# A two-layer decoder trunk on one core: feature-major input and memory, the first weights in quarters, the memory handled late in the first FFN

## The chip, the cores and the metric

The kernel runs on one core of one Trainium2 chip. The metric is the device time of one execution in microseconds (us). The core has a matrix engine (TensorE, PE in the profile), a vector engine (DVE), a scalar engine (ACT), GpSimd (POOL), and a sync engine (SP) that issues most of the DMAs. ACT and POOL can issue DMAs as well. Each engine works through its own instructions in order; semaphores tie the engines together.

## The reference

The input `x` is 256 tokens by 1024 features in f32, and there is a second input `mem` of the same shape. Two layers follow, each of four sub-layers with an RMSNorm ahead and one behind:

```
x += 1/2 * post(SwiGLU_1(pre(x)))          FFN, 1024 -> 2816 -> 1024
x += post(Mixer_l(pre(x)))                 layer 0: MLA | mLSTM, layer 1: sparse attention
x += post(CrossAttn(pre(x), norm(mem)))    4 heads over the 256 rows of mem
x += 1/2 * post(SwiGLU_2(pre(x)))
```

with `rmsnorm(x, g) = x * rsqrt(mean(x*x) + eps) * g` and `swiglu(x) = (silu(x @ wg) * (x @ wu)) @ wd`. The change concerns the first sub-layer (the first FFN) and the norm of `mem`, which the cross-attention of both layers uses.

## The kernel before, in words

**Products.** Each f32 operand is split in two: `hi` is the operand rounded to the matrix engine's f32r type, `lo` is the rest. A product is three terms: hi x hi, hi x lo, lo x hi. ACT makes `hi` (`hi_half`, a copy with a cast), DVE makes `lo` (`lo_half`, a subtraction). For the gate and up products of an FFN, `h_hi` and `h_lo` lie side by side in `h_both`, so one instruction of 512 columns does hi x (hi, lo) and one of 256 columns does lo x hi.

**Weights.** They come in chunks of 1 MB (128 partitions x 2048). SP loads a chunk into one of three raw slots (`raw` has two, `QT` is the third inside an FFN); ACT and DVE split it into a ring of four places, `w_ring`. `load(c)` on SP waits until the `lo` split of the slot's chunk before is done. An FFN has 11 pairs of gate and up chunks (G0.0, U0.0, ... in the text; the first digit is the sub-layer) and 11 down chunks (D0.0 ...). The order of work is written out by hand, on every engine: G0.0, U0.0, then for each pair p: G0.(p+1), U0.(p+1), D0.p. The middle eight turns are a hardware loop (`Fori`). At the end stand G0.10, U0.10, then D0.9 and D0.10 by token tiles, so that the first 128 tokens come out earlier.

**Input.** `pre` is not applied ahead of the first product: the gain goes into the input split, the row factor `rstd` is applied to the sums. It is put on a diagonal (`rdiag`), a product with a matrix of ones spreads it over the partitions (`row_factors` on PE, `rbc`), and `gate_scale` on DVE multiplies by it. The matrix engine needs features on the partitions, and `x` is loaded with tokens on the partitions, so PE turns the 16 blocks of 128x128 (`input_transposes`, L1072 of the profile). Ahead of them stand 13 transposes of nothing (`idle_turns`, L1253) and one that turns the norm gains (L1258). Then ACT makes `h_hi` (`input_hi`, L1579) and DVE `h_lo` (`input_lo`, L2243). `first_gate` runs G0.0 by halves of the features (L818 for `hi`, L823 for `lo`), `first_up` runs U0.0 (L861, L865).

**Memory.** `mem` is loaded with tokens on the partitions into `KTs` (`stage`), squared on ACT, scaled by DVE (L2234), turned by PE between U0.0 and G0.1 (`memory_transposes`, L1114) and split from PSUM in `m_hi` (ACT, `mem_hi`, L1698) and `m_lo` (DVE, `mem_lo`, L2429). Small parameter vectors come in nine small DMAs and are turned by one PE transpose (L1106) into `pcol`. The first user of the split memory is `fill(1)`, the product xk0.0, right behind the first FFN. Its weights are scaled by the memory's gain out of `pcol` while they are split: eight ACT instructions (L1543) and eight DVE instructions (L2205). Behind the FFN, `boundary` on DVE splits xk0.0 first, then multiplies the FFN's output by its gain (`gained`, L2257), adds it to x (`residual`, L2267), scales the rows (L2234), and makes the next `h_lo` (L2243), for which the first mixer product on PE (L755) waits.

**Order in the last pair of the first FFN.** ACT: `silu(10)`, the split of xk0.0, then `act_hi(10)`, the `hi` of the last activations. DVE: `gate_scale(10)`, the split of D0.10, `gate_up(10)`, `act_lo(10)`, then `boundary`. PE waits for `act_lo(10)` before the last down product (`act_ready(p)`).

## Time and profile before

| | |
|---|---|
| device time, median of three runs | 1104.31 us (1104.12 to 1104.64) |
| span of the profiled execution | 1102.8 us |
| PE busy | 1088.2 us, 99% of the span |
| DVE busy | 775.5 us, 70% |
| ACT busy | 562.1 us, 51% |
| POOL busy | 65.1 us, 6% |
| chain that ended last | PE 88%, DVE 6%, ACT 3% |

The span is that of one profiled execution, from its first to its last instruction; no device time of its own is given for that execution, and the median of the runs lies 1.5 us above its span. Line numbers are those of the kernel before. A matmul's row shows the time from its start to its modelled end; matmuls overlap, so the chain's rows, which follow the ends, are shorter than the durations of single ones.

### The profile page before, as it was taken

The page shows a single profiled execution, that of the slowest core. Times are in us where ns is not written, and L with a number is a line of the kernel's source. Part 1 is how long each engine was busy: PE and PEld are TensorE (multiplying, and loading weights), DVE is VectorE, ACT ScalarE, POOL GpSimd, SP SyncE. Part 2 cuts the span into 40 slices and gives each one's busy share as a digit, 9 for nine tenths or more (in the row PEclk, how much of TensorE's full clock was granted, in tenths as well). Part 3 has the DMA queues.
Part 4 walks back from the last instruction along what each step waited for, and adds up shares of the span by engine and source line. Part 5 has one row for each costly group of instructions (what it writes and reads, how often), then busy time and mean ns, then how long its engine had stood idle before and what let it go on. Part 6 is the DMA issues. An engine that isn't in the chain of part 4 may idle for free.

```text
span 1102.8 us, 16056 instructions
## 1 busy us (share of the span) xinstructions
PE 1088.2 (99%) x6175; PEld 941.6 (85%) x6175; DVE 775.5 (70%) x1023; ACT 562.1 (51%) x817; POOL 65.1 (6%) x168
## 2 busy tenths in 40 slices
PE   8999999999999999999999999999999999999997
PEld 7888888997889888888888888888987988888886
DVE  6867666763877677766768776677488768776674
ACT  7544344645667764434455443445465765443442
POOL 4000000210011010000010000001100101000000
PEclk9999999999999999999999999999999999999999
DMA  8655553571244356455426655552904435645540
GB/s 298 247 204 185 187 200 115 173 253 39 79 152 173 134 229 229 167 187 217 161 106 248 229 191 190 191 181 86 305 1 153 148 139 211 229 164 189 218 153 38
DMA packets 49399, 192.98 MB, mean 175 GB/s; under 512 B 3302, under 2 KB 24748, under 8 KB 31036
## 3 DMA queue, kind: packets, MB, share of 16 engines
q1 hardware_dynamic: 47932, 187.87, 48.3%
q0 software_dynamic: 1264, 4.25, 1.1%
q8 instruction: 38, 0.62, 0.2%
q14 instruction: 21, 0.17, 0.0%
q10 hardware_dynamic: 144, 0.07, 0.0%
HBM read 191.12 MB, written 1.05 MB: 174 GB/s over the span
## 4 chain that ended last, share of the span: by engine, by line
PE 88%; DVE 6%; ACT 3%; issue 1%; DMA 1%; POOL 0%; POOLq 0%; DVEq 0%; ACTq 0%
PE psum L878 28%; PE psum L978 21%; PE psum L877 12%; PE psum L1204 4%; PE psum L963 3%; PE psum L881 2%; PE psum L1195 1%; DVE w_ring L2211 1%; PE psum L742 1%; PE psum L744 1%; PE psum L743 1%; PE psum L767 1%; PE psum L769 1%; PE psum L768 1%; PE psum L818 1%
## 5 line engine op out<-in xcount | busy, mean ns | idle before, releaser
L878 PE MATMUL psum<-h_both,w_ring 128*128 128x512 f32 x1328 | 460.6, 396 | 0.0
L877 PE MATMUL psum<-h_both,w_ring 128*128 128x256 f32 x1162 | 324.0, 279 | 0.0
L2211 DVE TENSOR_TENSOR w_ring<-raw,w_ring 128x2048 fp32r<-128x2048 f32 x120 | 274.1, 2285 | 31.3 <-ACT w_ring L1547 31.0
L878 PEld LDWEIGHTS psum<-h_both,w_ring 128*128 128x128 f32 x1328 | 240.3, 188 | 46.5
L1547 ACT ACTIVATE w_ring<-raw 128x2048 fp32r<-128x2048 f32 x121 | 231.8, 1916 | 78.7 <-PE psum L978 48.6
L2335 DVE TENSOR_REDUCE work<-psum 128x256 f32<-128x512 f32 x174 | 118.4, 687 | 177.6 <-PE psum L878 176.5
L877 PEld LDWEIGHTS psum<-h_both,w_ring 128*128 128x128 f32 x1162 | 219.1, 189 | 7.4
L978 PE MATMUL psum<-w_ring,g_both 128*128 128x512 f32 x936 | 219.2, 389 | 0.0
L978 PEld LDWEIGHTS psum<-w_ring,g_both 128*128 128x128 f32 x936 | 175.7, 188 | 35.4
L1645 ACT ACTIVATE V<-work 128x512 f32<-128x512 f32 x44 | 27.8, 632 | 181.7 <-DVE work L2344 181.7
L2211 DVE TENSOR_TENSOR w_ring<-QT,w_ring 128x2048 fp32r<-128x2048 f32 x40 | 91.3, 2283 | 1.1 <-ACT w_ring L1547 1.0
L1649 ACT ACTIVATE g_both<-V 128x512 fp32r<-128x512 f32 x43 | 27.2, 633 | 120.5 <-DVE V L2351 120.5
L1547 ACT ACTIVATE w_ring<-QT 128x2048 fp32r<-128x2048 f32 x40 | 76.2, 1905 | 0.5 <-DMA QT<-in_ffn_w_down 0.5
L881 PE MATMUL psum<-h_both,w_ring 128*128 128x256 f32 x166 | 46.1, 277 | 0.0
L2243 DVE SCALAR_TENSOR_TENSOR h_both<-psum,gcol,h_both 128x128 fp32r<-128x128 f32 x128 | 34.6, 343 | 12.5 <-ACT h_both L1579 12.0
L638 POOL TENSOR_SCALAR part<-ss,eps_in 128x1 f32<-128x1 f32 x8 | 2.5, 312 | 692.4 <-ACT V L1569 692.4
L1579 ACT ACTIVATE h_both<-psum,gcol 128x128 fp32r<-128x128 f32 x128 | 35.1, 389 | 12.2 <-PE psum L1072 12.2
L881 PEld LDWEIGHTS psum<-h_both,w_ring 128*128 128x128 f32 x166 | 31.2, 188 | 6.8
L742 PE MATMUL psum<-h_both,w_ring 128*128 128x256 f32 x128 | 36.9, 288 | 0.0
L744 PE MATMUL psum<-h_both,w_ring 128*128 128x256 f32 x128 | 36.2, 283 | 0.0
L743 PE MATMUL psum<-h_both,w_ring 128*128 128x256 f32 x128 | 36.2, 283 | 0.0
L978 PE MATMUL psum<-w_ring,h_both 128*128 128x512 f32 x144 | 35.0, 396 | 0.3 <-DVE h_both L2174 0.2
(307 smaller groups left out, 1451.6 us busy)
## 6 DMA issues: line engine op xcount, KB each, us to landing
raw<-in_ffn_w_up SPq DMA_DIRECT2D x44, 1024.0 KB, 4.8
raw<-in_ffn_w_gate SPq DMA_DIRECT2D x43, 1024.0 KB, 4.8
QT<-in_ffn_w_down SPq DMA_DIRECT2D x40, 1024.0 KB, 4.7
raw<-in_ab_w_in SPq DMA_DIRECT2D x9, 1024.0 KB, 5.4
gain_row<-in_norm_g POOLq DMA_DIRECT2D x8, 512.0 KB, 5.0
raw<-in_ffn_w_down SPq DMA_DIRECT2D x4, 1024.0 KB, 4.7
raw<-in_xa_wk SPq DMA_DIRECT2D x4, 1024.0 KB, 4.8
raw<-in_ab_w_out SPq DMA_DIRECT2D x4, 1024.0 KB, 5.0
```

What stands on the lines that cost most here:

```text
L742: nc.tensor.matmul(o, wh, a_hi[:, k, :], start=(k == 0), stop=False)
L743: nc.tensor.matmul(o, wh, a_lo[:, k, :], start=False, stop=False)
L744: last = nc.tensor.matmul(o, wl, a_hi[:, k, :], start=False, stop=(k == KT - 1))
L877: nc.tensor.matmul(out_[:, 0:TOK], lo[:, k, o], h_hi[:, k, :], start=False, stop=False)
L878: last = nc.tensor.matmul(out_[:, :], hi[:, k, o], h_both[:, k].rearrange("p a n -> p (a n)"), start=(k == 0), stop=(k == KT - 1))
L881: nc.tensor.matmul(out_[:, 0:TOK], lo[:, k, o], h_hi[:, k, :], start=False, stop=False)
L978: last = nc.tensor.matmul(psum[:, 2 * t + half, :], a, w[:, k, 512 * half:512 * (half + 1)], start=(first and k == 0 and a is ah and w is hi),
L1204: last = nc.tensor.matmul(out_[0:rows, cols], a, b, start=(n == 0), stop=(n == len(terms) - 1))
L1547: nc.scalar.activation(w_hi[:, c % RING, 0:k * n], raw_at(c)[:, 0:k * n], ACT.Copy)\
L1579: ins = nc.scalar.activation(h_hi[:, k, P * t:P * (t + 1)], turned_at(s, t, k), ACT.Copy, scale=gain(s, k))
L2211: nc.vector.tensor_tensor(w_lo[:, c % RING, 0:k * n], raw_at(c)[:, 0:k * n], w_hi[:, c % RING, 0:k * n].bitcast(F32), ALU.subtract).then_i ...
L2335: nc.vector.tensor_reduce(dst[:, p % 2, TOK * j:TOK * (j + 1)], bank(name).rearrange("p (a n) -> p n a", a=2), AX.X, ALU.add)\
```

## The change

**Input.** The host lays out four more arrays: `first` (the gains of the first norm and `x`, feature-major), `gain_cols` (all norm gains by column), `mem_turned` (memory feature-major) and `columns` (the parameter vectors and `mem_norm_g` by column). The input and gain transposes on PE are gone. SP loads `first` in four DMAs of about 256 KB, ACT's queue loads G0.0 in four of 256 KB, and U0.0 comes in two halves on SP, ahead of `gcol`. `x` with tokens on the partitions is loaded behind G0.1, by two DMAs of 512 KB ahead of that of U0.1.

**First products.** ACT and DVE split input and weights quarter by quarter (two feature blocks each), out of SBUF and not out of PSUM. PE runs G0.0 in four steps and U0.0 in two (`by_steps`), and G0.1 by `first_up`, which starts on `hi` alone. 16 idle transposes stand ahead of it all.

**Memory.** Both layouts of `mem` are loaded at the end of the loop of the first FFN. The squares come ahead of the last but one pair on ACT. DVE puts the row factors on a diagonal, PE spreads them by one product (`memory_factors`, between G0.10 and U0.10), ACT copies them out, DVE multiplies the turned memory by them, ACT makes `m_hi` and DVE `m_lo`, all inside the last pair. PE's transposes of the memory and of the parameters are gone.

```diff
-            for t in range(NT):
-                sp.dma_start(x[:, t, :], A['x'][0, P * t:P * (t + 1), :]).then_inc(x_load[t], 16)
...
+            for q in range(4):
+                o = slice(KT + 2 * TOK * q if q else 0, KT + 2 * TOK * (q + 1))
+                sp.dma_start(work[:, o], A['first'][:, o]).then_inc(first_x_load[q], 16)
+            for half in range(2):
+                o = slice(4 * half, 4 * (half + 1))
+                dst = raw[:, 1, :].rearrange("p (k n) -> p k n", k=KT)
+                sp.dma_start(dst[:, o, :], chunks[1][1][0][:, o, :]).then_inc(raw_full[1] if half else first_up_load, 16)
+            sp.dma_start(gcol[:, :], A['gain_cols']).then_inc(gain_load, 16)
...
+            def load_memory():
+                sp.dma_start(stage, A['mem'][0].rearrange("(t p) n -> p t n", p=P)).then_inc(mem_load, 16)
+                sp.dma_start(m_raw[:, :, :], A['mem_turned']).then_inc(mem_turned_load, 16)
+                sp.dma_start(pcol[:, 0:NP], A['columns']).then_inc(par_load, 16)
...
-                for c in range(max(c0, 1), c1):
+                for c in range(max(c0, 2), c1):
                     load(c)
-                    if c == 1:
-                        sp.dma_start(stage, A['mem'][0].rearrange("(t p) n -> p t n", p=P)).then_inc(mem_load, 16)
-                        load_parameters()
+                    if c == 2:
+                        for t in range(NT):
+                            sp.dma_start(x[:, t, :], A['x'][0, P * t:P * (t + 1), :]).then_inc(x_load[t], 16)
...
+            def by_steps(name, ks, input_waits, hi_waits, lo_waits):
...
+                for step, (on_input, on_hi, on_lo) in enumerate(zip(input_waits, hi_waits, lo_waits)):
+                    if on_input:
+                        pe.wait_ge(*on_input)
+                    pe.wait_ge(*on_hi)
+                    for j in range(2):
+                        for k in range(ks * step, ks * (step + 1)):
+                            nc.tensor.matmul(outs[j][:, :], hi[:, k, P * j:P * (j + 1)],
+                                             h_both[:, k].rearrange("p a n -> p (a n)"), start=(k == 0), stop=False)
+                    pe.wait_ge(*on_lo)
...
+                def memory_factors():
+                    pe.wait_ge(mdiag_done, NT)
+                    filled("mrow", nc.tensor.matmul(take("mrow")[:, 0:TOK], ones[:, :], mdiag, start=True, stop=True))
...
# ACT, first FFN
+                if s == 0:
+                    act.wait_ge(mem_load, 16)
+                    for t in range(NT):
+                        square("m", t, stage[:, t, :], unread=m_hi[:, :, :].rearrange("p (t a) n -> p t (a n)", t=NT))
                 triple(p - 1)
                 nxt[0] = c0 + 3 * PAIRS - 1
                 split_to(nxt[0])
+                if s == 0:
+                    evacuate("mrow", mrow, bank("mrow")[:, 0:TOK])
                 silu(p)
+                if s == 0:
+                    mem_hi()
+                    act.wait_ge(par_load, 16)
                 split_to(c0 + 3 * PAIRS)
...
# DVE, first FFN
                 gate_scale(p)
                 split_to(nxt[0])
+                if s == 0:
+                    mem_scale()
...
                     gate_up(p)
                     act_lo(p)
+                if s == 0:
+                    mem_lo()
+                    dve.wait_ge(mem_split, 2)
                 boundary(s, C[f"D{s}.{p}"])
```

The first place is the start of ACT, which splits the first input and weights. In these rows `h_both` is the split input, `w_ring` the split weights, `KTs` the memory. Before:

```order
L1776 DMA work<-in_norm_g 128x128
L1560 ACT_TABLE_LOAD
L1560 ACTIVATE gcol<-psum 128x128
L1579 ACTIVATE h_both<-psum,gcol 128x128 x8
L1783 ACTIVATE w_ring<-raw 128x1024
L1579 ACTIVATE h_both<-psum,gcol 128x128 x8
L1787 ACTIVATE w_ring<-raw 128x1024
L1547 ACTIVATE w_ring<-raw 128x2048
L1569 ACTIVATE V,ss<-x_state 128x1024 x2
L1569 ACTIVATE V,ss<-KTs 128x1024 x2
L1547 ACTIVATE w_ring<-raw 128x2048 x2
L1698 ACTIVATE m_hi<-psum 128x512 x4
```

And changed:

```order
L1791 DMA raw<-in_ffn_w_gate 128x512 x4
L1795 ACT_TABLE_LOAD
L1795 ACTIVATE h_both<-work 128x256 x2
L1799 ACTIVATE w_ring<-raw 128x512
...
L1795 ACTIVATE h_both<-work 128x256 x2
L1799 ACTIVATE w_ring<-raw 128x512
L1803 ACTIVATE w_ring<-raw 128x1024 x2
L1553 ACTIVATE w_ring<-raw 128x2048
L1575 ACTIVATE V,ss<-x_state 128x1024 x2
L1553 ACTIVATE w_ring<-raw 128x2048
```

Eight passes over the input of twice the width stand in place of sixteen, in turn with the quarters of G0.0; the memory's six instructions are gone from here.

The second place is ACT at the end of the first FFN, from the split of D0.10 on (`g_both` is the last activations, `lat` holds the spread factors, `pcol` marks the split of xk0.0). Before:

```order
L1547 ACTIVATE w_ring<-raw 128x2048
L1645 ACTIVATE V<-work 128x512
L1543 ACTIVATE w_ring<-raw,pcol 128x256 x8
L1649 ACTIVATE g_both<-V 128x512
L1569 ACTIVATE V,ss<-psum 128x512 x2
```

And changed:

```order
L1553 ACTIVATE w_ring<-raw 128x2048
L1566 ACTIVATE lat<-psum 128x256
L1651 ACTIVATE V<-work 128x512
L1710 ACTIVATE m_hi<-KTs 128x1024 x2
L1549 ACTIVATE w_ring<-raw,pcol 128x256 x8
L1655 ACTIVATE g_both<-V 128x512
L1575 ACTIVATE V,ss<-psum 128x512 x2
```

The memory's two `hi` passes stand ahead of the split of xk0.0, and both ahead of the `hi` of the last activations.

The third place is DVE in the same stretch, from the split of D0.10 on. Before:

```order
L2211 TENSOR_TENSOR w_ring<-raw,w_ring 128x2048
L2335 TENSOR_REDUCE work<-psum 128x256 x2
L2351 TENSOR_TENSOR V<-V,work 128x512
L2356 TENSOR_TENSOR g_both<-V,g_both 128x512
L2205 SCALAR_TENSOR_TENSOR w_ring<-raw,pcol,w_ring 128x256 x8
L2257 TENSOR_TENSOR KTs<-psum,gain_row 128x512 x2
```

And changed:

```order
L2224 TENSOR_TENSOR w_ring<-raw,w_ring 128x2048
L2449 TENSOR_TENSOR KTs<-m_raw,lat 128x1024 x2
L2348 TENSOR_REDUCE work<-psum 128x256 x2
L2364 TENSOR_TENSOR V<-V,work 128x512
L2369 TENSOR_TENSOR g_both<-V,g_both 128x512
L2456 TENSOR_TENSOR m_lo<-KTs,m_hi 128x1024 x2
L2218 SCALAR_TENSOR_TENSOR w_ring<-raw,pcol,w_ring 128x256 x8
L2270 TENSOR_TENSOR KTs<-psum,gain_row 128x512 x2
```

Two passes over the memory stand ahead of the sums of U0.10, and two between the `lo` of the last activations and the split of xk0.0.

## Rows read from the trace of the kernel before

**Rows 1.** The page, part 1: busy time, share, instructions.

```profile
PE 1088.2 (99%) x6175; PEld 941.6 (85%) x6175; DVE 775.5 (70%) x1023; ACT 562.1 (51%) x817; POOL 65.1 (6%) x168
```

**Rows 2.** Chain of waits, 0 to 40 us: start, us, what.

```profile
9.64 3.63 PE psum L818 x8
...
14.27 1.84 PE psum L818 x8
...
17.07 1.84 PE psum L861 x8
...
22.65 1.75 PE psum L1114 x16
...
30.01 0.43 PE psum L1102 x2
...
30.63 0.43 PE psum L878
```

**Rows 3.** DMA view, 0 to 40 us: GB/s in slices of 1 us.

```profile
GB/s 0 20 264 395 394 279 229 348 459 430 406 397 446 214 6 139 352 434 377 410 393 451 451 181 60 84 352 418 393 303 131 385 442 82 8 0 0 131 147 434
```

**Rows 4.** Source view of L518, the two loads of x: ns each, first and last start.

```profile
L518 SPq DMA_DIRECT2D x_state<-in_x x2: 383/400/416, 0.8 to 1.2; - x2
...
DMA to landing us min/median/max: 4.0/4.4/4.9
```

**Rows 5.** Timeline, 0 to 40 us: start, us, engine, line, what, and releaser.

```profile
8.48 1.10 ACT L1783 ACTIVATE w_ring<-raw 128x1024 fp32r<-128x1024 f32 x1
...
14.24 0.36 SPq L550 DMA_DIRECT2D raw<-in_ffn_w_gate  x1
...
19.06 1.92 ACT L1547 ACTIVATE w_ring<-raw 128x2048 fp32r<-128x2048 f32 x1 [0.52 <-DMA raw<-in_ffn_w_gate]
...
26.79 2.27 DVE L2211 TENSOR_TENSOR w_ring<-raw,w_ring 128x2048 fp32r<-128x2048 f32 x1
...
36.26 3.79 PE L998 MATMUL psum<-w_ring,g_both 128*128 128x512 f32 x16
```

**Rows 6.** Source view of L1253, the idle transposes: ns min/median/max, first and last start.

```profile
L1253 PE MATMUL psum<-ident x13: 421/421/477, 1.7 to 4.4; 128*128 128x128 f32 x13
```

**Rows 7.** Source view of L1114, the memory's transposes, same columns.

```profile
L1114 PE MATMUL psum<-ident,KTs x16: 272/272/273, 22.5 to 24.1; 128*128 128x128 f32 x16
```

**Rows 8.** PE in stretches: busy (count), granted clock, DMA share, GB/s.

```profile
8.00:9.00 1.00, 0.00 (x0) 1.00 1.11 459
...
10.00:11.00 1.00, 1.00 (x4) 0.50 0.97 406
```

**Rows 9.** Timeline of ACT, 164 to 216 us.

```profile
182.49 3.29 ACT L1543 ACTIVATE w_ring<-raw,pcol 128x256 fp32r<-128x256 f32 x8
187.55 0.63 ACT L1649 ACTIVATE g_both<-V 128x512 fp32r<-128x512 f32 x1 [1.76 <-DVE V L2351]
```

**Rows 10.** Timeline of DVE, 164 to 216 us.

```profile
181.84 2.28 DVE L2211 TENSOR_TENSOR w_ring<-raw,w_ring 128x2048 fp32r<-128x2048 f32 x1
...
188.21 0.69 DVE L2356 TENSOR_TENSOR g_both<-V,g_both 128x512 fp32r<-128x512 f32 x1 [0.70 <-ACT g_both L1649]
188.82 3.25 DVE L2205 SCALAR_TENSOR_TENSOR w_ring<-raw,pcol,w_ring 128x256 fp32r<-128x256 f32 x8
193.62 1.47 DVE L2257 TENSOR_TENSOR KTs<-psum,gain_row 128x512 f32<-128x512 f32 x2 [1.55 <-ACT V L1569]
195.56 1.41 DVE L2267 SCALAR_TENSOR_TENSOR x_state<-KTs,rstd,x_state 128x512 f32<-128x512 f32 x2 [0.47 <-POOL rstd L642]
...
199.81 1.21 DVE L2224 TENSOR_TENSOR w_ring<-raw,w_ring 128x1024 fp32r<-128x1024 f32 x1
200.93 1.27 DVE L2257 TENSOR_TENSOR KTs<-psum,gain_row 128x512 f32<-128x512 f32 x2
```

**Rows 11.** Chain of waits, 180 to 220 us.

```profile
190.15 2.73 PE psum L978 x12
...
204.45 0.35 PE psum L755
```

More of the change, by code:

```diff
@@ L171, in cross @@
                     f"pT{u[2]}", f"pT{u[3]}", f"pv{u[2]}", f"pv{u[3]}"])
-    out.append("gains")
     ffn(0)
+    out.insert(out.index(f"U0.{PAIRS - 1}a"), "mrow")
     fill(1)
@@ L650, in _ @@
                 rms("pre0", t)
-            for t in range(NT):
-                rms("m", t)
             with nc.allow_non_contiguous_dma(reason="256 positions, 96 gate rows"):
@@ L671, in _ @@
             load_gain(0)
+            for t in range(NT):
+                rms("m", t)
             for s in range(SUBS):
@@ L849, in first_gate_by_tiles @@
                     filled(f"{name}{'ab'[j]}", products(j, 1, range(KT)))
+            def by_steps(name, ks, input_waits, hi_waits, lo_waits):
+                c = C[name]
+                k_, n = size(c)
+                hi, lo = (w[:, c % RING, 0:k_ * n].rearrange("p (k n) -> p k n", k=k_) for w in (w_hi, w_lo))
+                outs = [take(f"{name}{j}") for j in "ab"]
+                for step, (on_input, on_hi, on_lo) in enumerate(zip(input_waits, hi_waits, lo_waits)):
[7 more added lines that the diff above has]
+                    pe.wait_ge(*on_lo)
+                    for j in range(2):
+                        for k in range(ks * step, ks * (step + 1)):
+                            last = nc.tensor.matmul(outs[j][:, 0:TOK], lo[:, k, P * j:P * (j + 1)], h_hi[:, k, :],
+                                                    start=False, stop=(k == KT - 1))
+                        if k == KT - 1:
+                            filled(f"{name}{'ab'[j]}", last)
             def first_up(name):
@@ L927, in begin @@
                 out_ = fill(s, 0)
-                if s == 0:
-                    for half in range(2):
-                        for t in range(NT):
-                            input_transposes(s, t, [half])
-                    return
                 input_transposes(s, 1)
@@ L1247, in tile @@
                 return a[:, P * t:P * (t + 1)]
-            def idle_turns(n):
-                for _ in range(n):
-                    nc.tensor.transpose(psum[:, 3, 0:P], ident[:, :], ident[:, :])
             pe.wait_ge(const_done, 1)
-            idle_turns(13)
-            pe.wait_ge(gain_load, 16)
-            out_ = take("gains")
-            filled("gains", nc.tensor.transpose(out_[:, 0:P], grow[:, :], ident[:, :]))
+            nc.tensor.transpose(psum[:, 3, 0:P], ident[:, :], ident[:, :]).then_inc(down_done, 1)
+            for _ in range(15):
+                nc.tensor.transpose(psum[:, 3, 0:P], ident[:, :], ident[:, :])
             ffn(0)
@@ L1773, in cross @@
                 boundary(s, last)
[L1776 to L1789 removed]
+            for q in range(4):
+                o = slice(2 * q, 2 * q + 2)
+                dst = raw[:, 0, :].rearrange("p (k n) -> p k n", k=KT)
+                act.dma_start(dst[:, o, :], chunks[0][1][0][:, o, :]).then_inc(first_w_load[q] if q < 3 else raw_full[0], 16)
+            for q in range(4):
+                act.wait_ge(first_x_load[q], 16)
+                for k in (2 * q, 2 * q + 1):
+                    nc.scalar.activation(h_hi[:, k, :], first_x[:, k, :], ACT.Copy, scale=first_gain[:, k:k + 1])\
+                        .then_inc(first_h_hi, 1)
+                act.wait_ge(*((first_w_load[q], 16) if q < 3 else landed(0)))
+                o = slice(CH // 4 * q, CH // 4 * (q + 1))
+                nc.scalar.activation(w_hi[:, 0, o], raw[:, 0, o], ACT.Copy).then_inc(first_w_hi if q < 3 else split_hi, 1)
+            for half in range(2):
+                act.wait_ge(*(landed(1) if half else (first_up_load, 16)))
+                o = slice(CH // 2 * half, CH // 2 * (half + 1))
+                nc.scalar.activation(w_hi[:, 1, o], raw[:, 1, o], ACT.Copy).then_inc(split_hi if half else up_hi, 1)
+            nxt[0] = 2
+            split_to(2)
             for t in range(NT):
@@ L1792, in _ @@
                 square("pre0", t, x[:, t, :])
-            act.wait_ge(mem_load, 16)
-            for t in range(NT):
-                square("m", t, stage[:, t, :])
             split_to(3)
@@ L2692, in laid_out, with feature_major, columns, packed @@
     return np.ascontiguousarray(a)
+def feature_major(a):
+    return a.reshape(TOK, KT, P).transpose(2, 1, 0)
+def columns(a):
+    return a.reshape(-1, P).T
+def packed(inputs):
+    first = np.concatenate([columns(inputs['norm_g'][0, 0]), feature_major(inputs['x']).reshape(P, KT * TOK)], axis=1)
+    return {'first': first, 'gain_cols': columns(inputs['norm_g']), 'mem_turned': feature_major(inputs['mem']),
+            'columns': np.concatenate([columns(inputs[name]) for name in COLUMNS], axis=1)}
 def kernel(**inputs):
```

212 lines of the change are left out of this document (100 added, 112 removed).

## The prediction

> **What bounds the kernel now.** I read the page first: PE is busy 99% of the span and DVE 70% [rows 1]. So the end moves only where PE waits, works at half speed, or does work that is dropped. Next the chain of waits over the first 40 us [rows 2]: the first real product starts at 9.64, its first eight instructions take 3.63 us where the same eight take 1.84 later, the memory's transposes take 1.75 us of PE, and the first down product starts at 36.26 [rows 5]. Behind that PE doesn't wait until the end of the first FFN. So the head is worth up to what stands ahead of 36.26 beside 22.4 us of needed products (four chunks at twice 2.80, from 14.27 to 17.07). Then the timelines at the end of that FFN [rows 9, 10] and the chain there [rows 11]: PE gets its first mixer product at 204.45, and what it waits for is DVE's chain: split of xk0.0, gain, residual, next input. DVE is thus on the path in exactly the stretch to which the change moves the memory.
>
> **The head, part by part.** The time at which D0.0 can start decides, since all behind it follows at PE's pace.
>
> *Landing of the quarters.* A step of G0.0 needs 0.26 MB of x and as much of the weights. Summed over its slices, the DMA view [rows 3] gives 0.53 MB at 3.6 us, 1.05 MB at 4.95 and 2.10 MB at 8.4. The loads of x were issued at 0.8 and 1.2 and took 4.0 and 4.9 us [rows 4], so they landed at 4.8 and 6.1. Their bytes (with 0.06 MB of gains) had moved by 3.8 and 5.1. So landing comes 1.0 us behind the bytes. The first pair lands at 4.6, the last at 9.4. I take the old curve as it is, with its dip from 5 to 8 us, since the new pieces are no longer than the old ones.
>
> The trace cannot show two queues loading large pieces side by side. If they did not share, the first pair would land with its half of the bytes, at about 4.0, and the last at 6.0; I take the shared value. The Trainium skill, DMA: Bandwidth & Descriptors, section "Issuing engines are not separate DMA queues", says that transfers run on the same 16 DMA engines and interleave, whichever engine started them. By that the shared value holds; without it the last quarter would come 3.4 us earlier.
>
> *Splits.* The trace has no pass of exactly this kind at the start; the nearest rows are 0.41 us for 128x256 on ACT (3.29 for eight, rows 9) and on DVE (3.25, rows 10), and 0.63 and 0.69 for 128x512. A quarter costs ACT 2 x 0.41 + 0.63 = 1.45 and DVE 1.51; a quarter arrives every 1.6. They keep up. PE starts at 4.6 + 1.5 = 6.1 in place of 9.64. The last `lo` quarter is ready at 9.4 + 1.45 + 0.69 + 0.1 = 11.65.
>
> *The next chunks.* That split frees the raw slot, so SP issues G0.1 at 11.65 and no longer at 14.24. It took 4.8 us to land (14.24 to 19.06, rows 5): 16.45. Now x with tokens on the partitions (1.05 MB) stands ahead of U0.1 (1.05 MB) on the queue. At 0.42 MB per us (slices 8 to 13 and 16 to 23 of rows 3) both take 5.0: U0.1 lands at 21.45. ACT splits it in 1.92 and DVE in 2.27 [rows 5], with two handovers of 0.05: 25.75. U0.1 itself takes 36.26 - 30.63 = 5.63 [rows 2, 5]. **D0.0 starts at 31.4, so 4.9 earlier.**
>
> *PE's own way there.* Last step of G0.0 from 10.95 to 12.35; U0.0 to 17.95; G0.1 waits for its `hi` until 18.4, then between its two halves for `lo` (20.75), and ends at 24.5; row factors 0.43 [rows 2] and a bubble of 0.2; wait until 25.75. PE has 1.6 us of waits on this way. So the dropped 1.75 us of transposes, the parameters' transpose and the half-speed stretch are already in the 4.9 and may not be added: what is late next is U0.1, because of its load. The squares of x, 16 idle transposes (until 5.5, still ahead of 6.1) and `gcol` stand beside other work. If loads came sooner, PE would bind: 12.0 + 5.6 + 5.6 + 0.6 + 5.6 = 29.4, a gain of 6.8. That is the upper bound; the lower one comes from loads at 0.31 MB per us (slices 5 to 8): the last quarter lands 0.3 later, at 9.7, the 2.1 MB up to U0.1 take 6.8 in place of 5.0, and the gain is 2.8.
>
> *The loop.* Its loads follow the splits, all shift with PE. Nothing new. The 2.1 MB of memory come where the DMA queues are half idle. SP issues them ahead of G0.10, whose split is 7 us and more ahead of need. Cost: nothing. The squares (about 2 us on ACT) stand where ACT is waiting for a ring place; nothing either.
>
> **The end of the first FFN**, in the times of the kernel before.
>
> PE gets one f32 product more, 0.6 with its bubble (30.01 to 30.63, with the parameters' short transpose in it, rows 2). DVE, behind the split of D0.10 (181.84 + 2.2), multiplies the memory: two passes of 128x1024, at 1.12 each (199.81 to 200.93, rows 10): 186.4. ACT's two `hi` passes follow them: the second 186.45 to 187.55 (1.10, rows 5). Only then come the eight instructions of xk0.0, 3.29 us, which stood at 182.49 before, in free time; they end at 190.8. Only then `hi` of the last activations (before: 187.55): 191.45, and `lo` at 192.15 in place of 188.90 [rows 9, 10]. PE reaches that product at 190.15 + 0.6 and waits 1.4; the first 128 tokens are out at 192.2 + 2.73 = 194.9 [rows 11].
>
> DVE goes on with two `lo` passes of the memory (2.25): 194.4; xk0.0 3.25: 197.65; gain 1.27: 198.9. The residual, which started at 195.56, starts at 198.9 [rows 10]. PE's own delay (1.4 + 0.6) is shorter and has no say. Everything from there to the product at 204.45 is the same chain. **Loss 3.3.** Bounds: 0.6, if DVE's idle time (1.55 ahead of L2257) and ACT's took the new work in whole, and 4.5 = four passes of DVE, if none of it is hidden.
>
> **Sum.** -4.9 + 3.3 = -1.6. The span goes from 1102.8 to 1101.2. The median of the runs lies 1.5 above the span of the profiled execution, and I keep that distance: 1104.3 - 1.6 = 1102.7. A measurement of this kernel can tell about 0.2% (2.2 us) from no change, so this forecast is "within 0.2%".
>
> **Rivals.**
>
> *A. PE binds in the head.* The quarters land at an even 0.4 MB per us and U0.1 in time. For it: slices 2 to 4 and 8 to 13 of rows 3 are at 0.39 to 0.46, and the dip may be no property of these loads. Against it: x stands ahead of U0.1 whatever the rate. Gain 6.8, less 3.3: 1100.8. Chance 14%.
>
> *B. The end hides the memory.* ACT and DVE have idle time there. Against it: the order is fixed, and `hi` of the last activations stands behind the memory and xk0.0. Loss only 0.6: -4.9 + 0.6, 1100.0. Chance 13%.
>
> *C. Slower: the quarters land together.* Eight DMAs of two queues share the DMA engines; if these work on several at a time, the first quarter lands near the last, at 9.4. Then the four quarters of splits (5.8) come behind it: the last `lo` at 9.4 + 6.6 = 16.0 in place of 11.65, the gain sinks by 4.35 to 0.5, and with 3.3 the time is 1107.1. From a first landing at 6.65 on, the last `lo` is at 13.25 and the gain no more than the 3.3 of the end; each us later costs one. Against it: the two loads of x landed 1.3 apart, in order [rows 4]. Chance 8%.
>
> *D. The clock.* After a stretch with PE idle at 8 to 9 us the granted clock was 0.50, the 1.2 GHz level, from 10 to 13 [rows 8]. The change leaves PE idle only from 5.5 to 6.1, but with small waits between steps. Half speed for 3.3 us costs PE 1.65, and its waits ahead of U0.1 hold 1.6, so the price is 0 to 0.5: 1103.0. All of G0.0 at half speed would cost 5.6 and leave 4.0. Chance 13%. The idle transposes took 421 ns each at the start and the memory's 272 [rows 6, 7], though the granted clock reads full in both. The Trainium skill, TensorE: Matmul & The Clock Gate, Part 1, says that the default state is throttled and activity releases it. The rows on the transposes agree.
>
> **How the numbers follow.** The forecast gets 52%, with 1101.3 to 1104.3 for itself; A 14, B 13, C 8, D 13. The range takes in A and B, and the lower bound of the head (-2.8 + 3.3: 1104.8): 1099.6 to 1105.4. Faster by over 0.2%: A, B and 9 of the forecast's 52, so 0.36. Slower by over 0.2%: C but for its milder half, and the worst of D, 0.06. Within: 0.58.
>
> **What the profile would show.** Right: first product of G0.0 near 6.1; its last step near 11 to 12.5; U0.1's ACT split waits for a DMA until about 21.5; D0.0 starts near 31.4; at the end of the FFN `lo` of the last activations 3 us later against PE's G0.10 than before, PE idle over 1 us ahead of the last down product and again ahead of the first mixer product. Wrong in the head: first product after 7, or D0.0 before 30 or after 33. Wrong at the end: PE not idle there, or the distance from G0.10's start to the first mixer product grown by under 2 or over 4.5. Any change elsewhere than in the first 32 us and around 180 to 205 would make the whole reading wrong.

## The result, and the profile after

| | before | after |
|---|---|---|
| device time, median of 8 runs | 1104.16 us (1104.08 to 1104.64) | 1106.80 us (1105.04 to 1108.71) |
| ratio to before, 95% interval | | 1.0024 (1.0015 to 1.0033) |
| profiled execution: device time, span | span 1102.8 | 1106.68, span 1104.9 |
| PE busy, products | 1088.2 us, 6175 | 1084.2 us, 6146 |

The change makes the kernel slower by 2.6 us. The forecast was 1102.7 and the range ended at 1105.4: the prediction was wrong. The runs of the changed kernel also lie 3.7 us apart, those of the kernel before 0.6.

Both terms of the sum came out nearly as worked out. The chain of waits of the changed kernel, 0 to 40 us (start, us, what):

```profile
0.80 4.76 DMA work<-in_first
5.59 0.91 ACT h_both L1795 x2
...
15.67 0.33 SPq L552
...
16.04 9.43 DMA QT<-in_ffn_w_down
25.48 1.92 ACT w_ring L1553
...
35.28 2.30 DVE w_ring L2224
37.58 0.13 issue
37.70 0.49 PE psum L902
```

Its timeline (start, us, engine, line, what, and in brackets the idle time before and what ended it):

```profile
7.16 1.17 PE L865 MATMUL psum<-h_both,w_ring 128*128 128x512 f32 x4 [1.74 <-DVE h_both L2538]
...
11.95 0.33 SPq L552 DMA_DIRECT2D raw<-in_ffn_w_gate  x1
...
21.76 1.92 ACT L1553 ACTIVATE w_ring<-raw 128x2048 fp32r<-128x2048 f32 x1 [1.05 <-DMA raw<-in_ffn_w_up]
```

The first quarter landed at 5.56 and the first product ran at 7.16, in place of 9.64 [rows 2]. G0.1 was issued at 11.95 (forecast 11.65; before 14.24, rows 5), U0.1 was there at 21.76 (forecast 21.45), and D0.0 started at 31.76 in place of 36.26 [rows 5]: 4.5 gained. The last rows of the chain are new. G0.2 starts at 37.70, 5.94 behind D0.0, where it was 5.44 before (41.70 less 36.26): PE waits for DVE's split of its weights. The chain to that split goes through D0.0's load, which landed at 25.47. ACT splits D0.0 ahead of its copy of the row factors, and DVE needs the copy first. The gain at G0.2 is 4.0, and in the loop 3.93.

The end of the first FFN, timeline of DVE:

```profile
180.12 2.35 DVE L2449 TENSOR_TENSOR KTs<-m_raw,lat 128x1024 f32<-128x1024 f32 x2
...
187.31 0.69 DVE L2369 TENSOR_TENSOR g_both<-V,g_both 128x512 fp32r<-128x512 f32 x1 [2.92 <-ACT g_both L1655]
187.92 2.35 DVE L2456 TENSOR_TENSOR m_lo<-KTs,m_hi 128x1024 fp32r<-128x1024 f32 x2
190.31 3.26 DVE L2218 SCALAR_TENSOR_TENSOR w_ring<-raw,pcol,w_ring 128x256 fp32r<-128x256 f32 x8
193.49 1.28 DVE L2270 TENSOR_TENSOR KTs<-psum,gain_row 128x512 f32<-128x512 f32 x2
194.81 1.42 DVE L2280 SCALAR_TENSOR_TENSOR x_state<-KTs,rstd,x_state 128x512 f32<-128x512 f32 x2
```

and of ACT:

```profile
181.37 2.20 ACT L1710 ACTIVATE m_hi<-KTs 128x1024 fp32r<-128x1024 f32 x2 [2.71 <-DVE KTs L2449]
183.47 3.29 ACT L1549 ACTIVATE w_ring<-raw,pcol 128x256 fp32r<-128x256 f32 x8
186.67 0.61 ACT L1655 ACTIVATE g_both<-V 128x512 fp32r<-128x512 f32 x1
```

The order is the one that the prediction spells out: memory, then xk0.0, then `hi` of the last activations on ACT, for which DVE waits 2.92; then two passes of memory and eight of xk0.0 ahead of the gain. The first mixer product starts at 203.69 in the chain, against 204.45 [rows 11]. The change is 0.76 ahead there.

It is lost behind this. From here to the end nothing is changed in code, and up to 320 us the distance stays (-0.76 at the first mixer product, -0.74 at 318 us). The chain from 315 to 352 us, of the kernel before:

```profile
320.19 2.21 DVE w_ring L2211
322.42 4.78 DMA raw<-in_xa_wq
327.22 1.92 ACT w_ring L1547
```

and of the changed kernel:

```profile
319.45 2.21 DVE w_ring L2224
321.68 5.80 DMA raw<-in_xa_wq
327.51 1.93 ACT w_ring L1553
...
341.15 6.65 DMA raw<-in_xa_wv
```

This is the cross-attention of layer 0. A load of 1 MB is issued here only when the last split has freed a raw slot, and the chain runs through the load. Before, the load of xa_wv takes 4.75 (from 340.86). So the distance to the kernel before, read at ScalarE's and VectorE's instructions, goes from -0.76 to +0.29 behind xa_wq and to +2.18 behind xa_wv, and stays near that to the end (span +2.1). The DMA view of the changed kernel, 341 to 349 us, has a row that the kernel before does not have in that stretch:

```profile
q1 hardware_dynamic: 206, 1.30, 56.1%
q0 software_dynamic: 144, 0.52, 16.0%
q8 instruction: 1, 0.02, 0.7%
...
raw<-in_xa_wv SPq DMA_DIRECT2D x1, 1024.0 KB, 6.6
```

The same view in slices of 0.2 us, GB/s. Before, 341 to 349 us:

```profile
GB/s 0 0 0 0 369 287 0 0 246 410 614 246 369 573 328 410 492 369 410 266 451 389 348 471 430 287 82 21 0 0 0 143 20 0 102 164 348 369 471 389
```

and after:

```profile
GB/s 0 0 0 82 0 328 287 0 0 0 492 287 410 451 369 451 369 410 451 369 369 307 451 348 492 369 410 205 0 41 41 0 102 225 61 20 20 184 451 369
```

Before, the bulk (with the 0.5 MB of gains from POOL's queue behind it) ends near 346.4. After, it ends at 346.6, but single packets of 8 KB still trickle in at 41 GB/s and less: most of the load was there, and a share of it was late. The load's split waited for that share, until 347.8. In the packets of the trace the last four of this load start at 346.27, 346.58, 346.88 and 347.19 and take 0.31 each: they went one after the other.

Over the whole span the page counts them (queue, packets, MB, share of 16 engines):

```profile
q8 instruction: 38, 0.62, 0.2%
```

One packet is 16 KB and takes about 1 us (0.96 for the one at 341.65). In the kernel before, 879 products lie between the eight of them from 253.6 to 401.1 us: 126 for each, with their weight loads 251 instructions. None starts between 88.9 and 178.4 us; the second pass of the first FFN's hardware loop, which runs the instructions of the first pass again, lies in this stretch. I read these packets as the program of TensorE. The Trainium skill, Runtime: NRT & Kernel Launch, section "Instruction fetch mechanics", says that an engine's instruction memory is refilled in 16 KiB blocks of 256 instructions by a DMA queue of the sequencer's own, and that crossing a block's end is mostly hidden. The count agrees; whether it is hidden is what the experiments ask. The change issues 29 products fewer ahead of this place, 58 instructions, and so moves every block's place in the program. A second queue of the same kind, q14, carries blocks of 8 KB; in no run does one of them start during the two loads that are compared here.

### The profile page after: what moved, and what is told of

Its sections match the earlier page's. It is cut to its first block, busy times and chain, and to the rows that moved or that the text cites. A ratio compares the mean times of both kernels' runs of the same rounds, so it can differ in the third digit from the quotient of the medians.

```text
span 1104.9 us, 15985 instructions
## 1 busy us (share of the span) xinstructions
PE 1084.2 (98%) x6146; PEld 937.1 (85%) x6146; DVE 776.0 (70%) x1018; ACT 561.6 (51%) x809; POOL 67.5 (6%) x168
## 4 chain that ended last, share of the span: by engine, by line
PE 84%; DVE 8%; ACT 3%; DMA 2%; issue 2%; POOL 0%; POOLq 0%; DVEq 0%; SPq 0%; ACTq 0%
PE psum L902 27%; PE psum L997 21%; PE psum L901 12%; PE psum L1215 4%; PE psum L982 3%; DVE w_ring L2224 2%; PE psum L905 2%; PE psum L1206 1%; PE psum L748 1%; PE psum L747 1%; PE psum L746 1%; PE psum L773 1%; PE psum L771 1%; PE psum L772 1%; PE psum L1074 1%
## 5 line engine op out<-in xcount | busy, mean ns | idle before, releaser
L902 PE MATMUL psum<-h_both,w_ring 128*128 128x512 f32 x1312 | 455.3, 396 | 1.0 <-DVE w_ring L2224 1.0
L902 PEld LDWEIGHTS psum<-h_both,w_ring 128*128 128x128 f32 x1312 | 237.4, 188 | 47.6 <-DVE w_ring L2224 1.0
L901 PEld LDWEIGHTS psum<-h_both,w_ring 128*128 128x128 f32 x1148 | 216.4, 189 | 7.3
L1585 ACT ACTIVATE h_both<-psum,gcol 128x128 fp32r<-128x128 f32 x112 | 30.8, 387 | 11.6 <-PE psum L1089 11.6
L905 PEld LDWEIGHTS psum<-h_both,w_ring 128*128 128x128 f32 x164 | 30.8, 188 | 6.7
L2369 DVE TENSOR_TENSOR g_both<-V,g_both 128x512 fp32r<-128x512 f32 x43 | 29.5, 686 | 7.1 <-ACT g_both L1655 7.1
```

The costliest lines, as they stand in the source:

```text
L901: nc.tensor.matmul(out_[:, 0:TOK], lo[:, k, o], h_hi[:, k, :], start=False, stop=False)
L902: last = nc.tensor.matmul(out_[:, :], hi[:, k, o], h_both[:, k].rearrange("p a n -> p (a n)"), start=(k == 0), stop=(k == KT - 1))
L905: nc.tensor.matmul(out_[:, 0:TOK], lo[:, k, o], h_hi[:, k, :], start=False, stop=False)
```

## Experiments

Theory 1: a block of the program falls on a load that TensorE waits for. Theory 2: the loss belongs to the new inputs, their place in memory, or the new order of loads. The start of a packet in q8 is read from the trace.

### More idle transposes at the start

```diff
-            for _ in range(15):
+            for _ in range(30):
                 nc.tensor.transpose(psum[:, 3, 0:P], ident[:, :], ident[:, :])
```

> Edit: 30 instead of 15 idle transposes behind the first one, so 30 PE instructions (15 loads, 15 products) more ahead of everything; PE idles there anyway (5.4 to 7.2 us). Theory 1 (loads of PE's own code, one 16 KB packet per some 256 PE instructions, fall on the loads of xa_wq and xa_wv that the path waits for): each code load comes about 2.3 us earlier in the program, off both weight loads; these take 4.8 us each again instead of 5.8 and 6.7, the time falls by 2.9 to 1103.9 and the runs lie within 1 us. Theory 2 (the added input arrays move the others in HBM and make loads slower): no change, 1106.8 with the same spread.

Measured: 1104.77 us (1104.35 to 1106.05), ratio 1.0007 (0.9998 to 1.0016). The blocks start at 319.4 and 340.0, ahead of both loads, and the chain reads:

```profile
322.60 4.82 DMA raw<-in_xa_wq
```

xa_wv takes 4.75. From the first mixer product (204.61, before 204.45) to the end the distance to the kernel before no longer moves (+0.16, and +0.2 between the spans). The 2.9 us are gone, by nothing but added instructions. But the first block of all moved too, from 22.3 to 17.9 us, onto the load of U0.1, in its timeline of ACT:

```profile
23.12 1.92 ACT L1553 ACTIVATE w_ring<-raw 128x2048 fp32r<-128x2048 f32 x1 [1.43 <-DMA raw<-in_ffn_w_up]
```

That is 1.36 later than 21.76; U0.1 started at 27.42 and the head lost about 0.9 to it. The same fault, moved to the start. The expected 1103.9 was missed by this 0.9.

### The new inputs in the kernel before

The four extra arrays of the changed kernel are laid out and handed over, and nothing reads them.

```diff
+    for name, a in packed(inputs).items():
+        a = np.ascontiguousarray(a)
...
```

> Edit: the kernel before with the four new input arrays declared and passed, and used by nothing. Theory 1 (code loads): no change, 1104.2. Theory 2 (placement of the arrays in HBM): 1106 to 1107 with runs spread over 3 us.

Measured: 1104.05 us (1103.90 to 1104.31), ratio 0.9999 (0.9990 to 1.0008). The four arrays alone are not the cause, neither by their place in memory nor by being there.

### The memory a pair earlier

The row-factor product goes ahead of G0.10, DVE's and ACT's passes over the memory between the sums of the last pair.

```diff
-    out.insert(out.index(f"U0.{PAIRS - 1}a"), "mrow")
+    out.insert(out.index(f"G0.{PAIRS - 1}a"), "mrow")
...
+                elif s == 0:
+                    sum_half("U", p, up_sum, 0)
+                    mem_lo(0)
+                    sum_half("U", p, up_sum, 1)
...
+                    act_lo(p)
+                    mem_lo(1)
+                    dve.wait_ge(mem_split, 2)
...
-                if s == 0:
-                    mem_lo()
-                    dve.wait_ge(mem_split, 2)
```

> Edit: the changed kernel with its memory block a pair earlier: the factors' product ahead of G0.10, DVE's two multiplications around the first sum of G0.10, ACT's two hi passes ahead of the last silu, one lo pass between the sums of U0.10. By my reading of the end of the first FFN (the hi of the last activations queued behind the memory and xk0.0 on ACT, four DVE passes on the path, 3.2 us in all), the distance to the first mixer product shrinks by 2.4 us; the code loads stay where they are, so theory 1 gives 1104.4. The rival reading (the loss there is the extra PE product and the later y, not the order) gives no change, 1106.8.

Measured: 1104.55 us (1102.61 to 1105.00), ratio 0.9999 (0.9990 to 1.0009). The chain of 186 to 206 us has the first mixer product at

```profile
200.99 0.36 PE psum L759
```

3.46 ahead of the kernel before and 2.70 ahead of the changed one. The term for the end of the FFN is thus shown by undoing it: of 3.2 there remain about 0.5. No instruction was added, and the blocks still collide (322.1):

```profile
319.31 6.13 DMA raw<-in_xa_wq
```

This execution loses more here than the load's 1.35. From 318 to 353 us the distance to the kernel before goes from -3.47 to -0.87, by 2.6. PE idles 1.76 us ahead of the next transposes (start 331.81), and then its granted clock is 0.50, the 1.2 GHz level. PE in stretches (busy, granted clock, DMA share, GB/s):

```profile
331.00:332.00 1.00, 0.19 (x2) 1.00 0.51 180
332.00:333.00 1.00, 0.99 (x7) 0.75 1.02 434
333.00:334.00 1.00, 1.00 (x6) 0.50 0.87 369
```

In the kernel before and in both executions of the changed kernel the clock reads 1.00 here.

### Both together

The diffs of "more idle transposes" and of "the memory a pair earlier".

> Edit: both, the memory block a pair earlier and 30 idle transposes. Theory 1: 1106.8 - 2.9 - 2.4 = 1101.5, faster than the kernel before by 0.24%. Theory 2: 1104.4.

Measured: 1102.42 us (1102.06 to 1103.68), ratio 0.9987 (0.9978 to 0.9996). The blocks are at 316.6 and 337.9, xa_wq takes 4.74 and xa_wv 4.82; the first mixer product is at 201.73, since U0.1's load is again late in the head. That is 0.74 later than with the memory alone moved (200.99), most of the 0.9 by which the time is above the expected.

### Fewer idle transposes in the kernel before

```diff
-            idle_turns(13)
+            idle_turns(3)
```

> The kernel before, with 3 idle transposes at the start in place of 13 (20 TensorE instructions fewer; nothing else). Theory 1 (the program of TensorE is itself loaded in 16 KB pieces over the DMA engines, and a piece that falls on a load which TensorE waits for costs time): the piece at 339.8 in the kernel before comes about 1.6 us later, onto the load of xa_wv at about 341. That load takes 1 to 2 us longer than 4.75, and the distance from the second FFN on grows by 1 to 2: about 1105.5, with a wider spread of the runs. The piece at 315.6 goes to about 317 and still misses xa_wq. Theory 2 (the loss at xa_wq and xa_wv belongs to the new layout or order of the inputs): those loads take 4.8 and 4.75 as before, 1104.1 apart from what the start does. The start itself can change through the clock: it is read apart from this, by the shift at 300 us.

Measured: 1104.78 us (1103.92 to 1105.01), ratio 1.0003 (0.9994 to 1.0012). A miss for my arithmetic. The block of 315.6 moved to 319.1, but that of 339.8 stayed (339.3, with the whole program 0.4 earlier), and xa_wv took 4.65. In both kernels 4241 products are still to come when it starts, so 20 instructions fewer didn't move it in the program; why, no run shows. So a block's place can't be had by dividing instructions by a rate; it is read from runs. The early stretch is 0.4 shorter.

### Nine idle transposes later, on top of the memory a pair earlier

```diff
+                    if s == 0:
+                        for _ in range(9):
+                            nc.tensor.transpose(psum[:, 3, 0:P], ident[:, :], ident[:, :])
```

> The changed kernel with the memory block a pair earlier, and 9 idle transposes behind the row factors, where TensorE idles ahead of U0.1 (18 instructions more, from there on). Theory 1: pieces of the program come 1.5 us earlier at 320 and 341, off the loads of xa_wq and xa_wv (gap there back to the kernel before's), while the first piece stays at 22.3 and leaves U0.1's load at 21.8. So the head keeps its 4.0, the end costs about 0.6, and the loss at 320 to 350 is gone: 1104.2 - 4.0 + 0.6 = 1100.8 at best; 1101 to 1102, below the version with 15 more at the start (1102.4). Theory 2 (the loss at 320 to 350 is of the layout): 1104.5 as with the memory block alone.

Measured: 1102.08 us (1101.60 to 1102.76), ratio 0.9981 (0.9972 to 0.9990). The blocks are at 318.4 and 337.1, both loads are short (4.80, 4.75), and the head's block stays at 22.4. The nine took TensorE from 26.12 to 27.27, in the version without them U0.1 had started at 26.33: 0.7 of the 1.3 missing from "at best" is their price in this execution. It hangs on the clock: both executions ran at half clock from 9 to 11 us, which made PE late. In the next run's, at full clock, the nine are through at 26.16, when U0.1 starts, 0.1 behind the changed kernel's 26.06.

### The copy of the row factors first, on top of the last

```diff
-                split_to(c0 + 4)
+                if s:
+                    split_to(c0 + 4)
...
+                split_to(c0 + 4)
```

> As the last, and ScalarE copies the row factors ahead of its first pass of D0.0 in place of behind it, so that the first sums of pair 1 don't wait for the copy. The changed kernel stalls 0.49 us ahead of G0.2 (its slack there was 0.95 before). If that stall hangs on the copy: 0.5 us below the last run, 1101.4 if that has 1101.9. If it is another wait, the same as the last run.

Measured: 1101.62 us (1100.93 to 1103.11), ratio 0.9977 (0.9968 to 0.9986), the fastest version. D0.0 starts at 31.84, as early as in the changed kernel, and G0.2 at 37.28. That is 5.44 later, as in the kernel before, where the changed kernel has 5.94: the stall is gone. (The 0.49 of the expectation is the duration of G0.2's first row; what was lost is 0.50.) The two medians differ by 0.46, as expected, but that does not show the term. In the last run's profile D0.0 started at 32.70 and G0.2 5.44 behind it, so there was no stall to remove. What made D0.0 0.86 later there is the clock. PE in stretches, the last run:

```profile
9.00:10.00 1.00, 1.00 (x5) 0.50 1.05 426
```

and this one:

```profile
9.00:10.00 1.00, 1.00 (x7) 1.00 1.06 428
```

### A dose between

Eight more idle transposes at the start, with the memory a pair earlier.

```diff
-            for _ in range(15):
+            for _ in range(23):
```

> The memory block a pair earlier, and 8 more idle transposes at the start (16 instructions; the earlier run had 15). A dose between: by theory 1 the pieces at 322 and 343 come about 1.3 us earlier, to 320.8 and 342, so the one at xa_wq is at the edge of its load and that at xa_wv still on it: between 1102.4 and 1104.5, about 1103.3. Theory 2: 1104.5.

Measured: 1102.46 us (1102.10 to 1106.05), ratio 0.9992 (0.9983 to 1.0001). The blocks are at 320.5 and 339.3, xa_wq takes 4.79 and xa_wv 4.88: 16 instructions are enough, more than I expected of them. The head's block is at 18.7, again on U0.1, and TensorE idles 1.94 us ahead of U0.1. In this profiled execution (1104.0 us, 1.5 above the median) the clock then fell. PE in stretches (busy, granted clock, DMA share, GB/s):

```profile
26.00:27.00 1.00, 0.00 (x0) 1.00 0.70 75
27.00:28.00 1.00, 0.58 (x3) 0.96 0.16 31
28.00:29.00 1.00, 1.00 (x5) 0.50 1.01 134
29.00:30.00 1.00, 1.00 (x5) 0.50 0.67 270
```

Half clock is the 1.2 GHz level. With 15 more transposes TensorE idled the same 1.94 and the clock read 1.00 throughout. D0.0 came 7.27 behind U0.1's start (27.42 to 34.69), there 5.70 (27.42 to 33.12): the half clock cost 1.6. The eleven runs fall in two groups, six at 1102.1 to 1102.5 and five at 1103.9 to 1106.1, and the profiled one is of the upper group.

### The fault put into the kernel before

```diff
-                    for k in range(KT):
-                        for t in range(NT):
-                            a = TOK * (k % 2) + P * t
-                            last = nc.tensor.transpose(psum[:, k // 2, a:a + P], stage[:, t, P * k:P * (k + 1)],
-                                                       ident[:, :])
-                    last.then_inc(mem_full, 1)
+                    nc.tensor.transpose(psum[:, 0, 0:P], stage[:, 0, 0:P], ident[:, :]).then_inc(mem_full, 1)
...
-            idle_turns(13)
```

> The kernel before without its 13 idle transposes and with one of the memory's 16 transposes (15 left out: the memory that the attention reads is no longer the reference's). TensorE gets 56 instructions fewer, nearly the 58 fewer of the change; loads, order of the inputs and layout stay as before. Taking 20 away had left the piece of the program at 339.3. Theory 1, with the position read from the runs (the piece stays off xa_wv with up to 42 fewer, and falls on it with 58): here it falls on the loads as in the changed kernel: xa_wq 5 to 5.8 in place of 4.78, xa_wv 5.5 to 6.7 in place of 4.75, the distance from 300 us to the end grows by 1.5 to 3 against the control run with 30 fewer, and the runs spread by over 2 us. Theory 2 (it belongs to the change's layout or loads): both loads as before, the distance unchanged, spread under 1 us.

Measured: 1105.89 us (1104.82 to 1106.98), ratio 1.0015 (1.0006 to 1.0024). The inputs, their layout and the loads are those of the kernel before, and yet the chain has

```profile
322.40 5.79 DMA raw<-in_xa_wq
...
341.85 4.72 DMA raw<-in_xa_wv
```

with a block at 323.4 on the first load. The second block starts at 341.6, 0.2 us ahead of its load's issue, and costs nothing. So only the first half of the expected loss came, and the loss at xa_wv has not been brought about in the old layout.

### Its control

The first part of that diff alone, the 13 idle transposes kept.

> Control for the last: the same 15 of the memory's transposes left out (the memory that the attention reads is no longer the reference's), the 13 idle ones kept: 30 instructions fewer. By theory 1 the piece stays at about 339, off the loads, xa_wq 4.8 and xa_wv 4.75. The 1.6 us of transposes are gone from TensorE, which may give up to 1.6 at the start: 1102.6 to 1104.2, spread under 1 us. Theory 2 expects the same of both runs from 300 us on.

Measured: 1104.38 us (1103.81 to 1106.17), ratio 1.0005 (0.9996 to 1.0015). Blocks at 319.1 and 339.5, the loads take 4.77 and 4.75. Between the two profiles the distance grows by 1.0 from 300 to 353 us; xa_wq's load differs by 1.02. That is theory 1's mark. The spread is not: this run's executions lie 2.4 us apart, the last one's 2.2. So a wide spread has other sources too. The record points to the clock: the executions fall in two groups, six at 1103.8 to 1104.4 and five at 1105.7 to 1106.2. The mean granted clock of the five is 0.998 in each, that of the six 0.998 to 1.000. No profile of the upper group was kept, so this is not shown; "a dose between" had the same two groups, and there the profiled execution of the upper one shows a stretch at half clock that cost 1.6.

### Nine transposes in the changed kernel

The diff of "nine idle transposes later", nothing else.

> The changed kernel with nothing but 9 idle transposes behind the row factors, where TensorE waits for U0.1 (18 instructions more from there on). Theory 1: pieces of the program 2 us earlier at 320 and 341, the 2.94 lost there gone, the first piece left at 22.3: 1104.2 - 4.0 + 3.2 = 1103.4, up to 1104 if the added transposes delay U0.1 by 0.4 as they did with the memory block moved; the terms of the prediction would then sum as they should. Theory 2: 1106.8.

Measured: 1104.10 us (1103.91 to 1105.07), ratio 0.9999 (0.9990 to 1.0008). The blocks are at 321.2 and 340.2; the DMA view of 320 to 346 us has xa_wq at

```profile
raw<-in_xa_wq SPq DMA_DIRECT2D x2, 1024.0 KB, 4.7
```

and the chain xa_wv at 4.77. The changed kernel without its loss is 1104.1. In this profile G0.2 starts 0.67 later than in the changed kernel's (38.37, 37.70); how much of that is the nine transposes and how much the clock of the head is open, since the first four products took 2.04 us here and 1.17 there. Less up to 0.7, that leaves 1103.4 to 1104.1 for the terms that the prediction had. The runs lie 1.2 us apart.

### The changed kernel again

> The changed kernel itself, on the same chip as the three others. Theory 1: 1106.8 with a spread of 2 us and more, the pieces of the program on the loads of xa_wq and xa_wv in its profile; the length of those two loads differs between executions, since a 16 KB piece holds one of the 16 DMA engines for about 1 us at a slightly different time. Theory 2 has no reason for the spread.

Measured: 1106.63 us (1105.05 to 1108.09), ratio 1.0021 (1.0011 to 1.0030). Blocks at 322.8 and 341.2, and in the chain

```profile
321.85 5.52 DMA raw<-in_xa_wq
...
341.04 6.76 DMA raw<-in_xa_wv
```

Both loads differ by 0.1 to 0.3 from the first execution's (5.80, 6.65). The runs lie 3.0 us apart, and with the nine transposes 1.2, so most of the spread goes with the collision; how, the two profiles (spans 1104.9 and 1105.1) don't show. And the head differs. PE in stretches here:

```profile
9.00:10.00 1.00, 1.00 (x3) 0.50 1.03 418
10.00:11.00 1.00, 1.00 (x5) 0.50 1.02 411
```

In the first execution the clock reads 1.00 in both. D0.0 starts at 31.95 here and at 31.76 there, 0.2 later.

### All runs side by side

Instructions against the kernel before, counted as two for each product fewer; start of the block behind the load's issue; duration of the load.

| kernel | instructions | xa_wq: block, load | xa_wv: block, load |
|---|---|---|---|
| changed | -58 | +1.0, 5.80 | +0.55, 6.65 |
| changed, again | -58 | +1.0, 5.52 | +0.2, 6.76 |
| memory a pair earlier | -58 | +2.7, 6.13 | +4.3, 4.8 |
| before, fault put in | -56 | +1.0, 5.79 | -0.2, 4.72 |
| memory earlier, eight more | -42 | -1.2, 4.79 | -0.9, 4.88 |
| changed, nine later | -40 | -1.1, 4.7 | -0.5, 4.77 |
| memory earlier, nine later | -40 | -1.3, 4.80 | -1.0, 4.75 |
| the same, copy first | -40 | -1.2, 4.83 | -1.0, 4.89 |
| control | -30 | -3.0, 4.77 | -1.0, 4.75 |
| changed, 15 more | -28 | -3.2, 4.82 | -1.1, 4.75 |
| memory earlier, 15 more | -28 | -3.5, 4.74 | -0.7, 4.82 |
| before, ten idle fewer | -20 | -3.0, 4.7 | -1.1, 4.65 |
| before, new inputs | 0 | -6.9, 4.79 | -1.1, 4.71 |
| before | 0 | -6.8, 4.78 | -1.0, 4.75 |

A block that starts 0.2 to 2.7 us behind the issue lengthens the load by 0.7 to 2.0; one that starts 0.2 or more ahead of it, or 4.3 behind, adds at most 0.14. The sides are cleanly apart over kernels with the old and with the new layout, in one profiled execution of each row. The new loads and their order stay in "changed, nine later" and "changed, 15 more", and the loss is gone, so theory 2 has nothing left.

## Why the prediction was wrong

**The head, -4.9.** Right in its mechanism, measured -4.5 at D0.0. The first quarter took 4.76 from its issue and landed at 5.56, not 4.6, so the first product came 1.06 late, at 7.16. By the prediction's own signs a first product after 7 meant a wrong head; the landing of the first quarter was indeed mis-sized. It was caught up, since, as the prediction said, U0.1's load sets the end and not PE. G0.1's issue, U0.1's landing and D0.0's start were each 0.3 to 0.4 behind the forecast.

**Behind it.** A further 0.5 went at G0.2. Before, DVE's split for it was done at 40.75 and the product began at 41.70, a slack of 0.95. The split in the timeline of DVE of the kernel before:

```profile
38.47 2.28 DVE L2211 TENSOR_TENSOR w_ring<-raw,w_ring 128x2048 fp32r<-128x2048 f32 x1
```

The change brings PE there 4.5 earlier, but this split only 3.2 (35.28). The prediction let "all behind it follow at PE's pace" from D0.0 on and looked at no wait behind. With the row factors copied first the stall was gone (5.44 between D0.0 and G0.2, not 5.94).

**The end of the first FFN, +3.3.** Right, 3.2. The residual was forecast 3.3 later; less the 3.93 by which the loop ran ahead that is 194.93, measured 194.81. PE's wait ahead of the last down product was forecast as 1.4 and was 1.39.

**The step that failed** is the sum, "-4.9 + 3.3 = -1.6". It puts everything behind the product at 204.45 at nothing, and the prediction gives no reason for that; it only says at its end that any change elsewhere than in the first 32 us and around 180 to 205 would make the reading wrong. It did. ("The loop ... Nothing new" held: 4.0 at its start, 3.93 at its end.) The sum had no term for 29 products fewer except their time on PE. What they moved was the place at which blocks of the program are loaded, and two of them fell on loads that lie on the chain: +1.02 at xa_wq, +1.90 at xa_wv, together 2.9. With it the sum reads -4.5 + 0.5 + 3.2 + 2.9 = +2.1, the difference of the spans. The medians differ by 2.6; the profiled execution of before is not one whose device time is given, and single executions of the changed kernel lie up to 3.7 apart.

**The rivals.** None of them was it. PE did not bind in the head (A): it waited at 26.06 for U0.1. The end did not hide the memory (B): 3.2 lost. C did not come: the first quarter landed at 5.56, ahead of the 6.65 from which C costs anything, and ACT waited for none of the later ones. The clock (D) stayed at 1.00 in the head of this execution, even with 1.74 us of idle time ahead of the first product; in the second profiled execution of the same kernel it was 0.50 from 9 to 12 us, and D0.0 came 0.2 later, inside D's own 0 to 0.5. So D comes in some executions and is not the cause of the loss. The outcome was that of no rival, and on the side to which I had given 6%. What would have pointed to it stood in the view of the DMA queues of before, in the q8 row: 38 packets of 16 KB, and on the chain loads issued at 322.42 and 340.86 into empty queues, with nothing loaded ahead.

**What is shown, what is argued.** Shown: the loads' lengthening follows the block's place, and goes and comes with TensorE's instruction count alone, for xa_wq in both layouts, for xa_wv in the new one. Argued: that the 16 KB packets are TensorE's program, from their count, from their absence in the loop's second pass, and because edits of TensorE's instructions alone move them. The other blocks moved too and made no difference that can be told: from 353 us to the end the distance stays at 2.1 to 2.2. Open: by what path one packet of 0.96 us costs a load of 1 MB up to 2.0, and the spread of the runs, in which the clock has a part.

## What to carry to other kernels

A chain that runs through a load which is issued only when it is needed is exposed to whatever else uses the DMA engines, a block of program among them; look for such loads before adding up an edit's terms, and allow for each what it cost here, 0.7 to 2.0 us. An edit that adds or removes instructions far ahead can turn this on or off, so a result of some 2 us on a kernel of this size should be looked up in the trace at the place where it arises, and tried again with a few idle instructions more, before it is put down to the edit's idea. Look at the granted clock of each profiled execution before two of them are compared: two executions of one kernel differed in it here. Work moved into the last stretch of a stage can cost most of its own time: four passes of DVE, 4.7 us, cost 3.2 there and 0.5 a pair earlier.

## What the runs showed of the hardware

- A 16 KB block of program on one DMA engine lengthened a 1 MB load from 4.75 to as much as 6.76 us, twice its own 0.96 us. The Trainium skill, Runtime: NRT & Kernel Launch, section "Instruction fetch mechanics", calls the crossing of a block mostly hidden. The trace agrees for the other blocks, whose moves made no difference, and not for these two, nor for the one that fell on U0.1's load.
- When a block is loaded does not follow the instruction count evenly. The block at xa_wv started with 4236 to 4242 products to come, with 0 to 42 instructions fewer, and with 4209 to 4234 to come with 56 to 58 fewer. The block at xa_wq went from 4381 or 4382 to come (none fewer) over 4367 (20 to 30 fewer) and 4357 or 4358 (40 to 42) to 4340 to 4349 (56 to 58).
- The same idle stretch of TensorE, 1.94 us at 25.5 to 27.4, was followed by the full clock in one execution (15 more transposes) and by half clock, from 28 to 31 us, in another (a dose between), at a price of 1.6 us. The idle stretch ahead of the first product of the changed kernel, 1.74 and 1.81 us, was followed by the full clock in one execution and by half clock from 9 to 12 us in the other.
